# A two-layer decoder trunk on one core: the output product's first half moved ahead of the last head pair's finish, and unread products on TensorE

## The reference, cut to what matters

```python
for l in range(2):
    x = layer_norm(ALPHA * x + 0.5 * swiglu(x, ffn1_w_in[l], ffn1_w_out[l]))      # 1024 -> 2 x 2816 -> 1024
    f_r, f_s, f_g = split(x @ w_in[l])
    y_r = rwkv7_mixer(f_r, ...)   # 4 heads x 64, a recurrence over the tokens
    y_s = swa(f_s, ...)           # 8 query heads, 2 key heads, window of 128
    y_g = gdn_mixer(f_g, ...)     # 4 heads x 64, a conv of 4 taps, then a gated delta rule in chunks
    x = layer_norm(ALPHA * x + concat([y_r, y_s, y_g]) @ w_out[l])
    x = layer_norm(ALPHA * x + 0.5 * swiglu(x, ffn2_w_in[l], ffn2_w_out[l]))
```

## Time and profile before

| what | value |
|---|---|
| device time of three runs, us | 2911.15, 2923.39, 2926.39; median 2923.39 |
| the profiled execution's own time, us | 2920.07 |
| its span in the trace, us | 2917.9 |
| mean granted TensorE clock over the span | 0.927 of full speed |
| TensorE busy: products, weight loads | 2698.5 us (92%), 2519.8 us (86%) |
| VectorE, ScalarE, GpSimd busy | 1668.2 us (57%), 947.1 us (32%), 161.5 us (6%) |
| instructions | 59294 |

### The profile page before, as it was taken

How to read it: one execution, slowest core, us unless ns; L and a number is a source line. 1 busy time by engine, 2 the same in 40 slices (tenths; PEclk the granted TensorE clock), 3 DMA queues, 4 the chain that set the end, 5 groups by cost and what they waited for, 6 DMA issues and landing times.

```text
span 2917.9 us, 59294 instructions
## 1 busy us (share of the span) xinstructions
PE 2698.5 (92%) x23238; PEld 2519.8 (86%) x23238; DVE 1668.2 (57%) x2503; ACT 947.1 (32%) x1694; POOL 161.5 (6%) x168
## 2 busy tenths in 40 slices
PE   8999999978887899999999999999787879999996
PEld 8999999857665789999999999988666668999996
DVE  5666337654646466663356653467456655666534
ACT  4333224332212243332233332333222223333323
POOL 1030110000000010001100001100000001000011
PEclk9999999977867999999999999999777889999998
DMA  4852334200000323222222222431000022222221
GB/s 110 106 90 88 88 93 135 59 24 5 10 8 2 94 74 90 87 87 83 79 87 86 86 83 87 130 99 39 27 1 9 10 65 59 80 86 86 88 88 56
DMA packets 380501, 201.67 MB, mean 69 GB/s; under 512 B 41461, under 2 KB 376821, under 8 KB 379528
## 3 DMA queue, kind: packets, MB, share of 16 engines
q1 hardware_dynamic: 377928, 197.46, 23.2%
q0 software_dynamic: 2400, 1.82, 1.9%
HBM read 188.07 MB, written 13.34 MB: 69 GB/s over the span
## 4 chain that ended last, share of the span: by engine, by line
PE 78%; DVE 10%; issue 5%; ACT 4%; DMA 1%; SPq 1%; DVEq 0%; POOLq 0%; ACTq 0%; POOL 0%
PE ps L683 53%; PE ps L738 24%; DVE ar L1926 3%; DVE ar L1920 2%; ACT ar L1421 2%; DVE wl L1804 1%; ACT wh L1352 1%; PE ps L1012 1%; SPq L530 1%; DVE x L1920 1%; DMA raws<-in_ffn_w_in 0%; DVE ar L1956 0%; DVE xl L1911 0%; DVE ar L1923 0%; DMA raws<-in_w_in 0%
## 5 line engine op out<-in xcount | busy, mean ns | idle before, releaser
L1804 DVE TENSOR_TENSOR wl<-raws,wh 128x1024 fp32r<-128x1024 f32 x336 | 411.3, 1225 | 662.0 <-ACT wh L1352 657.8
L683 PE MATMUL ps<-xh,wh 128*128 128x272 f32 x2880 | 604.8, 291 | 18.5 <-DVE wl L1804 16.0
L738 PE MATMUL ps<-ar 64*64 64x64 f32 (+13 forms) x5408 | 484.1, 277 | 133.7 <-ACT ar L1421 37.8
L683 PE MATMUL ps<-xh,wl 128*128 128x272 f32 x2880 | 599.8, 290 | 0.0
L683 PE MATMUL ps<-xl,wh 128*128 128x272 f32 x2880 | 598.5, 289 | 0.0
L738 PEld LDWEIGHTS ps<-ar 64*64 64x64 f32 (+6 forms) x5408 | 359.7, 162 | 233.1 <-issue 66.1
L1352 ACT ACTIVATE wh<-raws 128x1024 fp32r<-128x1024 f32 x336 | 355.1, 1058 | 407.1 <-PE ps L683 376.4
L683 PEld LDWEIGHTS ps<-xh,wh 128*128 128x128 f32 x2880 | 457.5, 190 | 21.6 <-DVE wl L1804 18.0
L683 PEld LDWEIGHTS ps<-xl,wh 128*128 128x128 f32 x2880 | 457.9, 190 | 0.0
L683 PEld LDWEIGHTS ps<-xh,wl 128*128 128x128 f32 x2880 | 457.4, 190 | 0.0
L683 PE MATMUL ps<-hh,wh 128*128 128x272 f32 x1408 | 292.2, 289 | 0.0
(11 more groups left out here) (190 smaller groups left out, 2724.0 us busy)
## 6 DMA issues: line engine op xcount, KB each, us to landing
raws<-in_ffn_w_in SPq DMA_DIRECT2D x176, 512.0 KB, 3.6
raws<-in_ffn_w_out SPq DMA_DIRECT2D x64, 512.0 KB, 4.0
raws<-in_w_in SPq DMA_DIRECT2D x42, 512.0 KB, 3.5
raws<-in_ffn_w_out SPq DMA_DIRECT2D x32, 384.0 KB, 3.4
raws<-in_w_out SPq DMA_DIRECT2D x16, 448.0 KB, 4.0
x_kept<-x SPq DMA_DIRECT2D x2, 2176.0 KB, 10.1
x<-x_kept SPq DMA_DIRECT2D x2, 2176.0 KB, 7.9
ar<-in_consts SPq DMA_DIRECT2D x2, 1337.5 KB, 6.6
```

Source lines behind the costliest of these rows:

```text
L683: ins = pe.matmul(ps[:, bank + h, 0:n1 - h * NH], w[u % 2][:, k, :], a[:, k0 + k, h * NH:n1], start=(first and k == 0 and n == 0), stop=(l ...
L738: return pe.matmul(dst, lhsT, rhs, start=start, stop=stop, **kw)
L1804: dve.tensor_tensor(wl[u % 2][:, :, :], raw[u % 2][:, :, :], wh[u % 2][:, :, :].bitcast(F32), ALU.subtract).then_inc(sem("wl_done"), 1)
```

## The change

It has three parts. First, `keep_busy` is a new function on TensorE: it issues n products of `xh`, whose result nobody reads. In `prepare_gdn` it is called with 36 products of 272 columns, behind `banks_free` and ahead of the wait for `ge`. Second, `token_major` calls it ahead of each of the first four tiles' transposes, with two products of 128 columns. Third, on TensorE `mix` loses its empty first step and gets an empty one at its end, so that every half granule moves one step of the mix earlier, the first to M1; four waits stand ahead of it: for the attention's output, for the second head's output, and the two of `banks_free`. ScalarE's and VectorE's splits of granules 0 and 1 leave `mix` and go into `inverse` of pair 3, step P29: ScalarE's ahead of the corner copies, VectorE's behind its last operation of the inverse.

```diff
--- before.py
+++ after.py
@@ -176,6 +176,7 @@
 
 
 GATE_STEPS = 5
+TOKEN_FILL, PAIR_FILL = 2, 36
 PREPARE_STEPS = (27, 27 + GATE_STEPS, 30, 30)
 FINISH_STEPS = 22
 SAMPLE_STEPS = 7
@@ -959,6 +960,7 @@
                 def prepare_gdn(p):
                     q, c, U, ge = p.q, p.c, p.U, p.ge
                     banks_free(q)
+                    keep_busy(2, 0, NH, PAIR_FILL)
                     pe.wait_ge(sem("ge"), at(lay, "ge", c + 1))
                     for i in range(TILES):
                         ins = mm(ps[:, i // 2, i % 2 * 2 * P:(i % 2 + 1) * 2 * P], ge[:, i, :], cst("gd")[:, 0:2 * P])
@@ -1002,12 +1004,19 @@
                     yield from grams(p)
                     yield from inverse(p)
 
+                def keep_busy(bank, col, width, n):
+
+                    for _ in range(n):
+                        pe.matmul(ps[:, bank, col:col + width], xh[:, 2, 0:P], xh[:, 3, 0:width], start=True, stop=True)
+
                 def token_major(p, srcs):
 
                     for i in range(5):
                         o, w = tok_range(i)
                         if i == 4:
                             pe.wait_ge(sem("tok_copied"), at(lay, "tok_copied", 5 * p.q + 1))
+                        else:
+                            keep_busy(i, 3 * P, P, TOKEN_FILL)
                         for s, src in srcs:
                             ins = pe.transpose(ps[0:w, i % 4, s * P:(s + 1) * P], src[:, o:o + w], ident)
                         ins.then_inc(*tick("tok_t"))
@@ -1263,7 +1272,11 @@
 
                 def mix():
 
-                    yield
+                    pe.wait_ge(sem("attn_l"), at(lay, "attn_l", 2))
+                    pe.sem_inc(passed, 1)
+                    pe.wait_ge(sem("head_l"), at(lay, "head_l", 2))
+                    pe.sem_inc(passed, 1)
+                    banks_free(4)
                     for u in range(KC):
                         pe.wait_ge(sem("wl_done"), at(lay, "wl_done", BASE_WO + u + 1))
                         if u >= 2:
@@ -1272,6 +1285,7 @@
                         yield
                         mix_products(u, 4, KC - 1, 0, u % 2 * 2, False, True).then_inc(sem("mm_done"), 1)
                         yield
+                    yield
                     yield
 
                 head_pairs(prepare, finish, samples_attend, mix)
@@ -1642,6 +1656,8 @@
                         yield
                         yield
                     lo, hi = halves64
+                    for u in range(2 if q == 3 else 0):
+                        split(lay, BASE_WO, u)
                     for g in range(2):
                         pe_done("corner", g)
                         go(BB_[hi, 4 * g:4 * g + 4, :].rearrange("p m n -> p (m n)"), ps[hi, 2 + g, 0:4 * HD]).then_inc(*tick("inv_a"))
@@ -1719,8 +1735,6 @@
 
                 def mix():
 
-                    for u in range(2):
-                        split(lay, BASE_WO, u)
                     yield
                     yield
                     yield
```

## The result

The change makes the kernel slower: 2945.05 us in the median of 9 runs against 2923.39, ratio 1.0078, 95% interval 1.0051 to 1.0105. That is 22.8 us, where the sum had +2.2, and just outside the range. The profiled execution took 2948.19 us.

What follows compares the result with a forecast made beforehand. TensorE was taken to bound the kernel, through its work on the path and its clock, in the two token-mixing stages. -2.0 + 15.0 - 12.7 + 5.2 = +5.5 us on 2920.07 gave 2925.6 us; range 2902 to 2941.

Steps and rivals of the forecast that it cites:

- I count its 7.4 in full: Pair 2's token section, layer 1: the unread products bring the clock back, returning all 7.4 us.
- the 5.3 of pairs 0 and 1: Token sections of pairs 0 and 1, both layers: three tenths of a possible 17.6 us returned by clock, 5.3 us.
- The price of the clock: From pair 2's token sections in two layers: one slow microsecond, at 1.2 GHz, costs 0.42 us.
- 64 products at 0.235 (+15.0): Ahead of the token transposes: each narrow unread product lies on the path and costs 0.235 us, +15.0 us.
- The 36 products (-2.0): At the wait for `ge`: unread products raise the clock for the gate products, and VectorE regains its idle, -2.0 us.
- Pair 3 was put at nothing: Pair 3 has no such VectorE wait behind the gate products, so the 36 products gain nothing there.
- The move (+5.2): Product's first half and weight splits moved earlier: 0.8 at the start plus 1.8 at the end per layer, +5.2 us.
- 2.4 forecast: Last finish of the third head: VectorE's moved weight splits delay the head's output by 2.4 us.
- the 1.75 us wait at the end (1.8): End of the mixing stage: TensorE, with less work left, waits 1.8 us per layer for the last weights.
- From there TensorE is bound by its own work, the same as before, up to the end: Between the first recurrence step and the end of the mixing stage: no further time change until the last weight wait.
- the late head was set off against a shorter idle: Start of the recurrence: a head 2.4 us late, with TensorE's idle of 1.45 us becoming some 0.4, nets +0.8.
- The fill is not paid back: Rival, token sections: the 64 products cost 0.235 us or more each and return no clock; 2938 us, chance 0.15.

Runs made afterwards that it cites:

- e5: Kernel before plus only the 64 unread products ahead of the token transposes, made 272 columns wide instead of 128; ratio 0.9992, mean 2921.1 us.
- e10: The whole change, with its 64 token products 272 columns wide instead of 128; ratio 1.0006 to the kernel before, mean 2925.3 us.
- e2: Kernel before plus only the 64 unread 128-column products ahead of the token transposes; ratio 1.0089, mean 2943.2 us.
- e6: Kernel before plus only the token part, with six unread 128-column products per tile instead of two, 192 in all; ratio 1.0205, mean 2982.7 us.
- e3: Kernel before plus only the 36 unread products ahead of the wait for `ge`; ratio 0.9998, mean 2917.3 us.
- e9: The change without its token products: the moved product and the 36 products at `ge`; ratio 1.0031 to the kernel before, mean 2930.5 us.
- e12: Kernel before plus the 36 products at `ge` and 32 more of 272 columns in TensorE's wait before the third head's output; ratio 0.9991, mean 2918.7 us.
- e8: Kernel before plus only the moved product, with the weight splits left at the head of `mix`; ratio 1.0012, mean 2925.2 us.
- e13: Kernel before with only the first half granule moved a step earlier and the weight splits left in `mix`; ratio 1.0013, mean 2921.0 us.
- e4: Kernel before plus only the moved product and moved weight splits, no unread products; ratio 1.0063, mean 2936.5 us.

## Why the prediction was wrong

- **"I count its 7.4 in full", and the 5.3 of pairs 0 and 1 (-12.7).** This is the step that failed first. It took one difference between two layers of one trace for a property of pair 2. The second trace of the same kernel has it the other way round. In place of -12.7 the narrow products alone added 36 slow us: 15 of their own, which the price of the term below holds already, and 21 more, some +7. The price of the clock that the same rows gave, 0.42 us for a slow one, was right in kind; 104 executions give 0.35. By the rule of the Trainium skill ("TensorE: Matmul & The Clock Gate", section "What's actually happening"), activity releases the throttle. The runs agree for full-size products (slow time 402 in e5 and 364 in e10, against 427) and speak against it for the 128-column ones (464 in e2).
- **64 products at 0.235 (+15.0).** The unit was right for the first two of a section, 0.24 at half clock. Ahead of the later tiles a pair adds 0.28 to 0.34 us, so the term was mis-sized: 11 us of delay in all, 0.17 each. The 81 ns of the Trainium skill at full clock (same page, "Back-to-back issue gap") would be 0.16 at half, an estimate; from start to start the rows show 0.22 (in e6) to 0.24.
- **The 36 products (-2.0).** Mechanism right in pair 2, 1.3 to 1.5 us in layer 1, and the full clock for the gate products with it. Over the run no difference is measured. Pair 3 was put at nothing, and the stretch ahead of its transposes lasts 77 to 78 us with the products (e3, e9, e12) as without.
- **The move (+5.2).** Its signs all appeared: the head 2.7 us late (2.4 forecast), the 1.75 us wait at the end (1.8). The term was mis-sized because of the sentence "From there TensorE is bound by its own work, the same as before, up to the end". The work is the same in sum but not ahead of the last sums: one half granule more, 2.4 of the 3.0 us that e8 loses, stands there, and behind the sums runs a chain through ScalarE and the last weight split that less work on TensorE doesn't shorten: 8.07 us from the sums to the split's end before, 8.57 after (1029.98 to 1038.55). And the late head was set off against a shorter idle, as if the 24 products had filled it; they start behind the head, and the first steps end 1.1 us further behind it instead of 1.6 us nearer. So about 2.1 us go to the head at equal clock (2.7 and 3.7 us in the two layers, less 0.35 for each of the 2.8 and 3.6 slow us more), and 3.0 behind it, as e8 has it. Of these 3.0 the product in front of the recurrence is 0.6 (e13) and the half granule ahead of the sums the rest. That makes 5.1 per layer, 10 in all, where 12 was booked.
- **The rivals.** The one that came nearest is "The fill is not paid back", at 2938 with a chance of 0.15. It had the token price higher (15 against 11) and the move lower (5.2 against 10) than they are, so that its 2938 lies near the measured 2945 in part because two errors cancel, and it lacked what the narrow products take from the clock. No row of the trace before could have shown that; but a loss of clock through the narrow products belonged among the bounds: the text gave a reason against one only for the wide products.

Together: by e9 the token part is 13.7 of the 22.8 us. Its delay is 11, which leaves some 3 for the clock. The other 9 are the move with the products at `ge`; the rows of the move give 10. These terms are good to a few us each. The parts measured alone add up to 1.015 and not to 1.0078, 21 us more. Their slow time would add up to 451 us where the change has 428, which is 8 of the 21 at 0.35; the intervals of e2 and e4, 7 us to either side each, leave the rest open. What stays open too is why the clock rises later with narrow products. That the many slow us which e5, e10 and e12 save shorten the run so little is explained only in part: some fall in waits (shown ahead of pair 2), and in e5 and e10 the stretch from pair 3's turn to the third head lasts 34.9 to 38.2 us instead of 30.4 (33.2 and 33.9 with the move alone, e4, and the move is in e10 too).

## What to carry to other kernels

A clock that differs between two equal stretches of one trace is no evidence for a place; take a second trace of the unchanged kernel before such a difference enters a sum. Filler work on a path costs its time for certain, and its effect on the clock may have either sign: try it at full width first. When a step is moved ahead, count what then stands in front of each fixed chain behind it, not only the sum of the work.

## What was not expected of the hardware

At half clock, products of the fp32r type with weights of 128x128 followed each other in 0.22 to 0.24 us with 128 columns (six in 1.34 us in e6) and in 0.225 us with 272 in a long run: half the columns save next to no time in a stream, and 0.13 us for the two ahead of a section's transposes (0.49 against 0.62). Yet 64 of the narrow ones raised the slow time from 427 to 464 us and 192 to 527, with 15 and 42 of it their own, and 64 of 272 columns lowered it to 402, their own 17 included. And the same program spreads by 6.9 us from one execution to the next, along with its slow time, at 0.35 us for each slow microsecond.
